# The second block's f32 projections as three rounded products each, and three groups of transfers moved from GpSimd to SyncE

## What is computed

```python
sh1, sc1, g1, sh2, sc2, g2 = split(silu(c) @ ada_w + ada_b)        # and the same from c_ctx
h  = rmsnorm(x, norm1_g) * (1 + sc1) + sh1                          # 512 tokens
hc = rmsnorm(ctx, norm1_g) * (1 + csc1) + csh1                      # 256 context tokens
q, k, v, gu, gv, ga, gb = split(h @ w_in)     # widths 512 512 512 512 512 1024 1024
k_c, v_c = split(hc @ w_in[:, 512:1536])
y_a = neighborhood_attention(q, k, v, k_c, v_c, rpb)   # 8 heads, window of 8 rows x 16 columns, and the context
y_b = gelu(gu) * (ws @ layernorm(gelu(gv)) + bs)
m = sigmoid(ga) * (y_a @ w_proj_a) + sigmoid(gb) * (y_b @ w_proj_b)
x = x + g1 * (m @ w_out)
h2 = rmsnorm(x, norm2_g) * (1 + sc2) + sh2
x = x + g2 * peer_ffn(h2, wq, ...)            # queries h2 @ wq (1024 x 2048), top-16 keys, gated experts
```

## Time and profile before

| | us |
|---|---|
| median of 3 runs | 3439.38 (3439.19 to 3445.52) |
| the profiled execution, own time | 3443.26 |
| its span, first to last instruction | 3441.5 |
| second block's f32 projections on PE, 1326.93 to 1950.93 without the stage between | 502 |
| PE busy | 3331.1 (97%) |
| POOL busy | 1291.3 (38%) |
| DVE busy / ACT busy | 1675.6 (49%) / 943.1 (27%) |

### The profile page before, as it was taken

One profiled execution on the slowest core, in us unless ns is written; L12 is line 12 of the kernel. 1 busy time (PEld: TensorE's weight loads), 2 busy tenths in 40 slices (PEclk: granted clock), 3 DMA queues, 4 the chain that ended last, 5 costly groups with the idle time before them and its releaser, 6 DMA issues.

```text
span 3441.5 us, 38600 instructions
## 1 busy us (share of the span) xinstructions
PE 3331.1 (97%) x14734; PEld 1976.0 (57%) x14734; DVE 1675.6 (49%) x3436; ACT 943.1 (27%) x1431; POOL 1291.3 (38%) x711
## 2 busy tenths in 40 slices
PE   7999999998999999999999899999999999999998
PEld 5877775677456884544643444466666444444443
DVE  5433796557464442002521299844443055566664
ACT  2011226424451011102301222333333232322222
POOL 4664479455005661211301134333333333344331
PEclk9998999999999999999999999999999999999999
DMA  3222221022313222222012343344444476655561
GB/s 132 98 98 77 74 101 31 29 83 100 107 67 114 98 98 74 75 94 78 24 74 73 109 161 146 147 184 183 187 194 192 171 255 210 205 196 195 196 209 60
DMA packets 137457, 429.89 MB, mean 125 GB/s; under 512 B 9088, under 2 KB 77824, under 8 KB 114176
## 3 DMA queue, kind: packets, MB, share of 16 engines
q1 hardware_dynamic: 120784, 350.20, 28.6%
q10 hardware_dynamic: 7200, 68.68, 4.8%
q0 software_dynamic: 9360, 9.50, 1.1%
HBM read 358.10 MB, written 73.40 MB: 125 GB/s over the span
## 4 chain that ended last, share of the span: by engine, by line
PE 49%; DVE 1%; ACT 0%; POOL 0%; issue 0%; DVEq 0%; ACTq 0%
PE bank L884 13%; PE bank L885 13%; PE bank L886 13%; PE bank L795 7%; PE bank L907 3%; PE bank L1022 0%; POOL work L2196 0%; PE bank L494 0%; PE bank L515 0%; DVE rs L1542 0%; DVE hF L1546 0%; DVE work L1901 0%; ACT work L1346 0%; ACT rs L1084 0%; PE bank L877 0%
## 5 line engine op out<-in xcount | busy, mean ns | idle before, releaser
L2196 POOL TENSOR_TENSOR work<-ring,work 128x4096 bf16<-128x4096 f32 x64 | 531.7, 8308 | 1003.2 <-ACT work L1346 1003.2
L884 PE MATMUL bank<-work 128*128 128x512 bf16 x2048 | 777.1, 379 | 11.6 <-POOL work L2196 8.7
L885 PE MATMUL bank<-work 128*128 128x512 bf16 x2048 | 777.2, 379 | 0.0
L886 PE MATMUL bank<-work 128*128 128x512 bf16 x2048 | 777.0, 379 | 0.0
L2027 DVE TENSOR_TENSOR work<-hF,work 128x512 bf16<-128x512 f32 x128 | 300.6, 2348 | 250.4 <-ACT work L1430 247.3
L2217 POOL CAST w_parts<-ring 128x1024 fp32r<-128x1024 f32 (+4 forms) x160 | 174.3, 1089 | 620.3 <-DMA ring<-in_wstream 164.2
L2219 POOL TENSOR_TENSOR w_parts<-ring,w_parts 128x1024 fp32r<-128x1024 f32 (+4 forms) x160 | 394.6, 2466 | 12.8
L795 PE MATMUL bank<-hF,ring 128*128 128x512 f32 x768 | 334.9, 599 | 11.8 <-ACT hF L1093 11.0
L884 PEld LDWEIGHTS bank<-work 128*128 128x128 bf16 x2048 | 200.7, 98 | 246.6 <-issue 13.3
L886 PEld LDWEIGHTS bank<-work 128*128 128x128 bf16 x2048 | 200.6, 98 | 242.3 <-issue 1.1
L885 PEld LDWEIGHTS bank<-work 128*128 128x128 bf16 x2048 | 200.5, 98 | 235.0 <-issue 0.8
(11 more groups left out here) (280 smaller groups left out, 4653.8 us busy)
## 6 DMA issues: line engine op xcount, KB each, us to landing
ring<-in_wstream SPq DMA_DIRECT2D x129, 2048.0 KB, 7.6
hidden<-hF ACTq DMA_DIRECT2D x32, 1024.0 KB, 3.9
gates<-work ACTq DMA_DIRECT2D x16, 2048.0 KB, 8.3
hF<-hidden SPq DMA_DIRECT2D x32, 1024.0 KB, 6.6
work<-gates SPq DMA_DIRECT2D x32, 1024.0 KB, 10.2
rpb_tiles<-in_rpb POOLq DMA_DIRECT2D x192, 16.0 KB, 2.3
work<-rpb_tiles POOLq DMA_DIRECT2D x24, 128.0 KB, 2.3
ring<-in_wstream SPq DMA_DIRECT2D x4, 576.0 KB, 4.0
```

Source lines behind the costliest of these rows:

```text
L884: pe.matmul(out, a(0), b(0), start=(start and k == 0), stop=False)
L885: pe.matmul(out, a(0), b(1), start=False, stop=False)
L886: mm = pe.matmul(out, a(1), b(0), start=False, stop=(stop and k == n - 1))
L2196: nc.gpsimd.tensor_tensor(SPLIT[:, p, 1, :], ring[:, p, :], SPLIT[:, p, 0, :], ALU.subtract).then_inc(lo, 1)
```

## The change

The four projections become three rounded products. The chunk list and the list of rounded stages grow; `second_inputs`, `merge_branches` and `key_queries` take the place of `project_many`, and `d_out` uses the existing `project_features`. The k weights of a chunk serve the tokens and then the context; the v weights serve 4 + 2 token tiles at once. ACT writes the rounded input instead of the shifted one, and DVE takes the rest (shift added and rounded part subtracted in one instruction), two tiles behind. For the experts `hF` is still wanted in full after `d2`: ACT writes it behind the rests. In `neighbourhood` ACT and DVE round the branches as they come; in `merge` DVE adds by tiles. The `meet()` calls behind `neighbourhood` and `merge` are gone, and buffers have moved.

On POOL, `first_biases` (memset and the bias of the first two heads) stands ahead of `a_out1`; the mask, the v rows and the windows are issued by SP, the windows in 8 transfers of 256 KB instead of 32 of 64 KB.

```diff
-          ("a_in1", 32), ("a_out1", 8)]
+          ("a_in1", 32), ("a_out1", 8), ("d_q", 36), ("d_pa", 8), ("d_out", 8), ("d_wq", 16)]
...
@@ SyncE, behind each ring load
+                if (name, m) == ("a_out1", 0):
...
+                            sp.dma_start(D_MASK[16 * r:16 * r + 16, v, :], const_d[qc:qc + 16, kc:kc + 32])\
+                                .then_inc(signal("n_mask_in"), 16)
+                if (name, m) == ("d_ga", 0):
+                    sp.wait_ge(signal("d_q_taken"), 18)
+                    sp.dma_start(v_rows.rearrange("(t p) n -> p t n", p=P), D_VR).then_inc(signal("n_rows_out"), 16)
+                if (name, m) == ("d_pb", 0):
+                    sp.wait_ge(signal("n_rows_out"), 16)
+                    sp.wait_ge(signal("parts_used"), CHUNK["d_pa"])
...
@@ TensorE
+            def feature_group(out, w, hi, lo, tiles, opening=None):
+                for k in tiles:
+                    if opening is not None:
+                        pe.wait_ge(signal("rounded"), opening + k + 1)
+                    pe.matmul(out, w[0][:, k - tiles[0], :], hi[:, k, :], start=(k == tiles[0]), stop=False)
+                    pe.matmul(out, w[1][:, k - tiles[0], :], hi[:, k, :], start=False, stop=False)
+                for k in tiles:
+                    if opening is not None:
+                        pe.wait_ge(signal("rest_made"), opening + k + 1)
+                    mm = pe.matmul(out, w[0][:, k - tiles[0], :], lo[:, k, :], start=False, stop=(k == tiles[-1]))
+                return mm
...
+                features(0)
+                features(1)
+                tokens(own + [(ctx_rounded, ctx_rest, t) for t in range(2)])
+                tokens(own)
+                tokens(own)
+                for m in range(5, 9):
+                    features(m)
...
+            def merge_branches():
+                for m in range(2):
+                    for n in range(8):
+                        c, g = CHUNK["d_pa"] + 4 * m + n // 2, 8 * m + n
...
+                        mm = feature_group(bank[:, n, :], w, branch_rounded, rest, range(4 * m, 4 * m + 4),
+                                           ROUND["d_pa"] + 4 if g == 0 else None)
...
@@ ScalarE, norm d1 and d2
-                        act.activation(hF[:, k, :], hF[:, k, :], ACT.Identity, bias=ada[:, 0, c + k:c + k + 1])\
-                            .then_inc(signal("normed"), 1)
+                        act.activation(out[:, k, :], hF[:, k, :], ACT.Identity, bias=ada[:, 0, c + k:c + k + 1])\
+                            .then_inc(signal("rounded"), 1)
+                    if tag == "d2":
+                        for k in range(KT):
+                            act.wait_ge(signal("rest_made"), ROUND["d2"] + k + 1)
...
@@ VectorE, neighbourhood
+                    if 8 <= n < 12:
+                        rest_branch(n - 4, n - 8)
+                    if n >= 3 * NT and n % (2 * NT) == NT + 2:
+                        rest_branch(n // (2 * NT) - 1, n // (2 * NT) + 3)
                 finish(NA_HEADS - 1)
-                meet()
+                rest_branch(3, 7)
@@ VectorE, merge
                         v.tensor_tensor(gate_[:, n, :], gate_[:, n, :], bank[:, n, :], ALU.mult).then_inc(taken, 1)
-                dve.wait_ge(taken, 16)
-                v.tensor_tensor(D_M, D_SGA, D_SGB, ALU.add)
-                meet()
+                        if m == 1:
+                            dve.wait_ge(taken, 9 + n)
+                            v.tensor_tensor(D_M[:, n, :], D_SGA[:, n, :], D_SGB[:, n, :], ALU.add)\
+                                .then_inc(signal("d_merged"), 1)
+                            if n:
+                                rest_merged(n - 1)
+                rest_merged(KT - 1)
@@ GpSimd
             weight_parts("a_in1", 8, KT, 512)
+            first_biases()
             weight_parts("a_out1", 2, KT, 512)
-            neighbourhood_operands()
-            pool.wait_ge(signal("normed"), KT * 6)
+            weight_parts("d_q", 2, KT, 512)
+            weight_parts("d_q", 3, KT, 512, 2, 2, 8)
+            weight_parts("d_q", 4, KT, 512, 0, 5, 20)
+            neighbourhood_bias()
+            pool.wait_ge(stage_over, 3 * MEET_D)
+            weight_parts("d_pa", 2, 4, 1024, per=256)
+            weight_parts("d_out", 2, KT, 512)
+            weight_parts("d_wq", 4, KT, 512)
+            pool.wait_ge(signal("normed"), KT * 5)
             split_input()
             split_lo()
```

More of the change, by code:

```diff
@@ L1337, in neighbourhood, with merge @@
                         exps(n + 2)
-                meet()
+                    if n < 4:
+                        round_gating(n)
+                    if n >= 2 * NT and n % (2 * NT) == 3:
+                        round_pair(n // (2 * NT) - 1)
+                round_pair(3)
+            def merge():
+                for k in range(KT):
+                    act.wait_ge(signal("d_merged"), k + 1)
+                    act.activation(d_rounded[:, k, :], D_M[:, k, :], ACT.Copy).then_inc(signal("rounded"), 1)
             def split_hi(turn, p):
@@ L1488, in _ @@
             neighbourhood()
-            meet()
+            merge()
             norm("d2")
-            take_many("d_wq", [(m, j == 3, R_Q[:, 4 * m + j, :], ACT.Copy) for m in range(4) for j in range(4)])
+            take_many("d_wq", [(R_Q[:, g, :], ACT.Copy) for g in range(16)])
             key_scores()
```

338 lines of the change are left out of this document (190 added, 148 removed).

## The result

The changed kernel took 3359.97 us in the median of four runs (3357.05 to 3376.89), the kernel before 3440.51 beside it: a ratio of 0.9774 with a 95% interval of 0.9757 to 0.9791. It is faster by 2.3%, where 2.8% were forecast: 17 us slower than the forecast of 3343, at the slow end of the range (3361). A second comparison gave 3365.16 (3356.10 to 3368.72, six runs) and a ratio of 0.9750 [0.9723, 0.9777].

What follows compares the result with a forecast made beforehand. PE, busy for 97% of the span, was taken as the bound, with its f32 projections in the chain. Savings of 104.0 - 1.4 - 3 - 3.5 = 96.1 us gave a median of 3343 us, range 3333 to 3361.

Steps and rivals of the forecast that it cites:

- 53.4 + 11.2 + 18.5 + 20.9: Second block: us saved on input projections, merge, output (with its seam) and queries, in sum 104.0 us.
- the 5.50 taken from rows 4: All four projections: a rounded group of 24 matmuls takes 5.50 us, as between two first-block groups, 0.229 us a matmul.
- rival 2: Merge and output: POOL's chunks let DVE instructions past, taking 6.4 us each, 14 us more: 3357; chance 0.11.
- rival 4: Ring behind SP's waits: a slot or two late by up to 9.5 us each, 3352 to 3362; chance 0.06.
- Nothing, with 2 us of cover by the upper bound: Windows ahead of values: 2 MB need at most 19 us, values begin 21.1 us behind the input projections, so no loss.
- if values wait for the windows: Ahead of the values products: a sign that would show the prediction wrong; it expected no wait there.
- The first group behind a norm: Input projections and queries: the first group, paced by ACT's rounding and DVE's rest at low clock, takes 9.0 us.
- rival 5: First groups of d1, d2 and behind merge: clock stays at 1.2 GHz, 3 x 2.5 us: 3351; part of the forecast.
- End of merge: Second half of merge: DVE's two-operand instructions and POOL's chunks take turns; 3.5 us lost, bounds 0 and 6.3.
- if the seam ahead of the output is as long as it was: Between merge and output: a sign that would show the prediction wrong; the old seam of 5.25 us should go.
- the 1.4 us for biases: Start of a_out1: memset and six bias loads between POOL's chunks make PE wait, 1.4 us lost.
- Neighbourhood: Neighbourhood loop: POOL's first two merge chunks hold up DVE's scaling and with it PE; 3 us lost, bounds 0 and 7.

Runs made afterwards that it cites:

- bias_late: The changed kernel with GpSimd's zeroing and six first bias loads put behind the first block's output projection's chunks: 3378.49 us in one execution.
- win32_again: Second execution of the changed kernel with the value windows in 32 transfers of 64 KB instead of 8 of 256 KB: 3370.18 us.
- win16: The changed kernel with the value windows in 16 transfers of 128 KB (two rows each) instead of 8 of 256 KB: 3393.09 us in one execution.

## Why the prediction was right or wrong

The direction, the bound and most of the size held: PE's products set the time, and the four projections gave 53.4 + 11.2 + 18.5 + 20.9 in the sum and lie within a few microseconds of it in the table. Away from the seams the rounded group took 5.44 to 5.52 us, against the 5.50 taken from rows 4. Neither rival that set the slow end of the range came true: POOL's chunks never held PE up inside merge, output or queries (rival 2), and no ring slot did (rival 4). That the measured median (3359.97, as a ratio 0.9774) lies at that end (3361, as a ratio to 3439.38 0.9772) is no merit of theirs; other terms brought it there.

- **The step that failed** is "Nothing, with 2 us of cover by the upper bound", for the windows. The bound was no bound: from the first issue to the last landing the windows took 26.9 us, not 19. Rows 11 show 1 MB that goes out in one transfer with an outer dimension of 128, beside a ring load; its 9.5 us are 110 GB/s with start and landing in them. I carried this duration over to another shape, and so took the size of a transfer for what sets its time. The four-row windows moved at some 100 GB/s, and start and landing came on top. A nearer row stood in the kernel before, whose 32 window transfers of 64 KB went out one per 0.5 us (1456.0 to 1471.5) and landed after 2.1 us each. The diff has 8 with an outer dimension of 4, and I read that as fewer issues alone. It cost 6.1 us in the profiled execution. The 2.3 us of clock come on top only against the kernels without the wait; the kernel before got its clock back as late behind its first values product. The prediction did say what would refute it: "if values wait for the windows".
- **The first group behind a norm** was mis-sized at 9.0 us: it took 10.3 at the input projections (1325.77 to 1336.03) and 12.3 at the queries (1770.83 to 1783.13), and never less than 10.2 in the eleven profiles of rounded kernels. Two things are in it. I argued that the number of DVE instructions ahead of the last rest is the same, 16. But in rows 5 the eight scaled tiles came first; now scalings (L1646) and rests (L1664) alternate from the fourth tile on, so that PE's first 16 products get a tile every 1.32 us. The timeline of DVE alone, before, ahead of rows 5:

```profile
1085.99 5.39 DVE L1546 SCALAR_TENSOR_TENSOR hF<-xF,cols,rs 128x512 f32<-128x512 f32 x8
```

and in the changed kernel, ahead of the input projections:

```profile
1326.78 0.75 DVE L1646 SCALAR_TENSOR_TENSOR hF<-xF,small,rs 128x512 f32<-128x512 f32 x1
1327.44 0.74 DVE L1664 SCALAR_TENSOR_TENSOR rest<-hF,ada,d_rounded 128x512 fp32r<-128x512 f32 x1
```

Those 16 products took 8.4 us instead of 5.9, the last eight 1.8 instead of 3.1: 1.2 us in all. No edit tests this; it is read from the rows. The rest is **rival 5, "PE starves at the low clock"**, which was counted with the forecast but not in its sum: at the queries, with the clock at 0.50, the last eight products took 3.4 us and the first 16 8.9, together 2.0 more. The second group there took 5.75 us and the others 5.44 each, 0.5 less than forecast in all, which leaves the 2.8 missing.
- **End of merge**: right mechanism, and nearly the right size for it: I had 3.5 us, and the two waits are 2.58 + 1.19 = 3.8. But the first output group took 5.8 more than the groups behind it, because behind the waits the clock had fallen (0.53 from 1715.3 to 1718.3) and its last eight products took 3.2 us (1715.27 to 1718.50) instead of 1.8. This is rival 5 again, "once behind merge". The old seam was 5.25 us, so by the prediction's own sign ("if the seam ahead of the output is as long as it was") it did not go; it moved into the first group. What makes DVE late is seen in its rows: its three operations stand in one queue, and a stretched rest or addition also delays the next tile's multiplication, which is itself not stretched.
- **`a_out1`**: the 1.4 us for biases ahead of it came as 1.29. Missing was the second wait, 1.26 us at the fifth group. I had costed the context's rests at nothing without looking at who splits chunks beside them. It is what rows 8 show, in the other direction: 3 us of DVE's two-operand work held up POOL, and POOL's 1.9 us of spare time absorb only part.
- **Neighbourhood**: 3 forecast, 2.6 measured, from waits of 0.33 to 0.73 us on the scaling. The size was right in part by luck: that it is POOL's first two chunks was not. Most of these waits lie ahead of the chunks, where rests and head copies meet POOL's bias arithmetic.
- **Covers that held**: `split_input` (key scores to the experts' end 1489.3 against 1489.9), the masks and v rows on SP, and POOL's time per chunk inside all four runs of groups.

Together: 6.1 + 2.8 + 2.8 + 1.6 + 1.3 = 14.6 us less gained than forecast, -0.4 at the neighbourhood, and 3.9 + 0.6 by which this execution was shorter elsewhere: 9.7 of the 9.9 us missing. With the windows' wait and the end of merge removed the kernel took 3345.51 us, a ratio of 0.9715 where 3343 is 0.972. This does not make the forecast right: that version also lacks the 3.5 us that the forecast had put down as lost at the end of merge.

## What to carry over

Take the duration of a transfer only from one with the same outer dimension on both sides, and look at the DMA share beside its rate: 0.2 over a transfer that something waits for was here a fault in its shape. When an order of instructions changes, count what stands ahead of each input that is waited for, and not only ahead of the last. When GpSimd is given steady work, list VectorE's operations with two SBUF operands beside it, in both directions; an operand in PSUM took an operation out of the collision here, and it ran no slower for it (0.68 to 0.70 us). Compare executions stretch by stretch where totals scatter by more than the effect.

## What the runs showed of the hardware

The same 2 MB in pieces with an outer dimension of 2, 4 and 32 moved at 50, 100 and 140 GB/s, the last limited by 0.46 us per issue on SP; with two rows each, SP took 35.61 us to issue 16 transfers, 2.2 us each, so the issue itself took longer where the transfers were slow.

Executions of the same code differ in the granted clock. In the stretch from 350 to 400 us, which the change does not touch, the changed kernel's first profile and then that of `bias_late` have, with PE equally busy:

```profile
350.00:400.00 50.00, 47.02 (x199) 33.43 (x198) 34.86 (x84) 18.15 (x36) 16.32 (x10) 1.00 0.19 74
```

```profile
350.00:400.00 50.00, 47.02 (x134) 27.78 (x134) 21.81 (x47) 17.26 (x34) 7.25 (x5) 0.69 0.08 35
```

199 matmuls against 134 in the same 50 us. 0.31 of 50 us is 15.5 of the 20 us by which this execution reached `a_out1` late. `win32_again` has 0.66 in the same stretch, `win16` 0.69.
